# One decoder layer on one core: prompt keys of two heads in one 128-column product, the sixth latent block in two column halves, the first cached page on a semaphore of its own

## The chip, the cores and the metric

One Trainium2 chip, one of its NeuronCores. The metric is the time of one execution of the program on the device, in microseconds (us). Three runs of the kernel before were taken; their median is the number to compare with.

## The reference, cut to what matters

One decoder layer for 256 prompt positions and 8 single-token samples that share all weights. The part around the change is the latent attention:

```python
h = rmsnorm(x, lw['g_norm_mix']) * (1.0 + scale_m) + shift_m
p = jnp.einsum('ntd,de->nte', h, lw['w_in'])
q = mla_queries(p[..., OFF_Q:OFF_KV], pos, lw['g_q_lat'], lw['w_uq'], lw['g_qk_q'])
c_kv = rmsnorm(p[..., OFF_KV:OFF_KR], lw['g_kv_lat'])
k_rope = apply_rope(p[..., OFF_KR:OFF_CB], cos, sin)
...
def mla_keys(c_kv, k_rope, w_uk, g_qk_k):
    k_nope = jnp.einsum('...tc,chd->...thd', c_kv, w_uk)
    k_rot = jnp.broadcast_to(k_rope[..., None, :], k_nope.shape[:-1] + (QK_ROPE,))
    return rmsnorm(jnp.concatenate([k_nope, k_rot], axis=-1), g_qk_k)
```

With D_MODEL 1024, a query latent of 384, a key and value latent of 256, 8 heads, 64 unrotated and 32 rotated components per head. Each sample also attends to 8 cached pages of 128 latent rows. The layer ends with 64 routed experts of 3 MB each (float32), all of which are streamed from device memory.

## The kernel before, in words

All activations lie with features on the partitions and the 264 tokens (256 + 8) along the free axis. Everything is float32; each product in the program is recorded as two weight loads and two matmuls. Five engines run five programs that are written by hand and meet at semaphores. `STAGES` (L59) lists all products in the order in which TensorE makes them; each takes the next of four PSUM banks, and its number n gives the bank (n % 4) and how often it has been used. TensorE's `enter(n)` (L678) waits until the bank's last contents have been read, `full[n % 4]` tells the reader that it is filled, and `free[n % 4]` that it is read.

The order around the change is:

- **Early pages** (L416, L731, L1366, L1728). While the first weights load, the keys' squared lengths of 16 cached pages are made: SyncE issues the page loads in groups (`EGROUP`, L50), each group with one semaphore; TensorE waits for a group at its first page, and multiplies each page (2 products of 512 columns, 4 matmuls on record) by `wuk`; ScalarE squares, VectorE sums per head. Group 0 is pages 0 and 1 with `wuk`; group 1 is pages 2 and 3; group 2 is pages 4 and 5. Between them TensorE makes chunks of the conditioning (`ada_item`, L704, four column groups of 32 at once).
- **Latent blocks** (L763 to L778, stage `in0`). Six blocks of the combined projection, each 8 products of 264 columns over the 8 feature tiles of `hT`: three of queries, two of keys and values, and the sixth, the 32 rotated key components and their swapped copy, 64 output columns that are written to partitions 64 to 127. ScalarE copies each bank out (L1402, L1405) and squares the first five (L1411). Later VectorE rotates the sixth (`krT`, L1791 to L1793), after the variance of the query latent (L1786) and before the scaling of the query latent (L1797), which TensorE waits for ahead of stage `q`.
- **Prompt keys** (L824 to L831, stage `k`). For each of 8 heads 2 products of 64 output columns into a bank of its own; ScalarE copies each (L1449), and when all are there squares all heads in one instruction (L1455). TensorE goes on with four transposes (`ada_fold(6)`, L722), the sums of the squared queries (`qsum`), the values (`v`), and then the sums of the squared keys (`ksum`, L842), which wait for L1455.
- **After that** come the rest of the projection, attention with the cached pages, the branches, and the experts in pairs. SyncE's queue holds all large loads in program order, each behind a wait for TensorE to be done with the ring slot or chunk that it overwrites (L403, L408, L447, L548).

In the experts' `up` (L1236) two experts share one bank, each with 64 output columns, one on partitions 0 to 63 and one on 64 to 127, and the program goes from one to the other at each product.

Of the kernel before, what the change touches and what calls it, by code (L numbers as in the profile page):

```python
# [6 lines left out]
ALU = mybir.AluOpType  # L7
ACT = mybir.ActivationFunctionType
# [6 lines left out]
P = 128  # L15
D = 1024
DT = D // P
NP_ = 256
NS = 8
NT = NP_ + NS  # L20
NC = 1 + NS
H = 8
NOPE, ROPE = 64, 32
QK = NOPE + ROPE
QL, KL = 384, 256
QT, KT_ = QL // P, KL // P
# [18 lines left out]
T_Q, T_KV, T_CB, T_CC, T_CH, T_U, T_V = 0, 3, 5, 9, 13, 17, 21  # L45
# [1 line left out]

NPK = 6
EARLY = NS * (NPG - NPK)
EGROUP = (0, 2, 4, 6, 8, 10, 12, 16)  # L50

KNOW = []
for _q in range(NS):
# [2 lines left out]
BRANCH = []  # L56
for _m in range(DT):
    BRANCH += ([(f"bg{_m + 2}", 3)] if 0 < _m < DT - 2 else []) + [(f"bo{_m}", 3)]
STAGES = [("ek0", 2), ("ek2", 2), ("ada0", 1), ("ek4", 2), ("ek6", 2), ("norm1", 1), ("ada1", 1), ("ek8", 2), ("ada2", 1),  # L59
# [3 lines left out]
          ("ada10", 1), ("in_v2", 1), ("in_v3", 1), ("ada11", 1), ("know0", NPK // 2), ("self", 1), ("qlat", 1),  # L63
          ("know0b", 2), ("qlatT", 1), ("know0c", 1),
# [4 lines left out]
BASE = {}  # L69
# [110 lines left out]
def build(nc, A, O):  # L180

    with ExitStack() as ctx:
# [9 lines left out]
        hT = sb("hT", [P, DT, NT])  # L192
        xs = sb("xs", [P, 2, D + E])
        sq = xs[:].rearrange("p a c -> p (a c)")[:, 0:DT * NT].rearrange("p (k t) -> p k t", k=DT)
        pT = sb("pT", [P, NTILE, NT])
# [11 lines left out]
        krT = sb("krT", [P, 2, NT])  # L207
# [6 lines left out]
        kT = sb("kT", [P, H, NT])  # L214
# [12 lines left out]
        wuk = sb("wuk", [P, KT_, H * NOPE])[:]  # L227
# [118 lines left out]
        free = [sem(f"bank_free{i}") for i in range(4)]  # L346
# [330 lines left out]
        def _(pe):  # L677
# [14 lines left out]
            def mm(out, lhsT, rhs, start, stop):  # L692
                return nc.tensor.matmul(out, lhsT, rhs, start=start, stop=stop)  # L693
# [72 lines left out]
            w = part(0, 0, DT, 704)  # L766
            for m in range(6):
                n = BASE["in0"] + m
                t = enter(n)
                for k in range(DT):  # L770
                    if m == 0:
                        pe.wait_ge(s["h1"], k + 1)
                    if m < 5:
                        last = mm(t[:, 0:NT], w[:, k, m * P:(m + 1) * P], hT[:, k, :], k == 0, k == DT - 1)
                    else:
                        last = mm(t[NOPE:P, 0:NT], w[:, k, 640:704], hT[:, k, :], k == 0, k == DT - 1)
                last.then_inc(full[n % 4], 1)
            through(n, 0)  # L778

# [32 lines left out]
            for h in range(H):  # L812
                n = BASE["q"] + h
                t = enter(n)
                for k in range(QT):
                    last = mm(t[:, 0:NT], wuq[:, k, h * P:(h + 1) * P], pT[:, T_Q + k, :], k == 0, k == QT - 1)
# [5 lines left out]

            ada_item(6)
            pe.wait_ge(s["ckv"], 1)  # L824
            for h in range(H):
                n = BASE["k"] + h
                t = enter(n)
                for k in range(KT_):
                    last = mm(t[0:NOPE, 0:NT], wuk[:, k, h * NOPE:(h + 1) * NOPE], pT[:, T_KV + k, :],
                              k == 0, k == KT_ - 1)  # L830
                last.then_inc(full[n % 4], 1)  # L831
            ada_fold(6)
            pe.wait_ge(s["sqh"], 1)
# [1 line left out]
            for b in range(2):  # L835
                n = BASE["v"] + b
                t = enter(n)
                for k in range(KT_):
                    last = mm(t[:], pT[:, T_KV + k, b * P:(b + 1) * P], wuv[:, k, :], k == 0, k == KT_ - 1)
# [45 lines left out]
            n = BASE["self"]  # L885
            t = enter(n)
# [4 lines left out]
            n = BASE["qlat"]  # L891
            t = enter(n)
            for hf in range(2):
                for j in range(4):
                    h = 4 * hf + j
                    last = mm(t[32 * j:32 * j + NS, hf * KL:(hf + 1) * KL], qsg[0:NOPE, h, :], wukT[:, h, :], True, True)
# [3 lines left out]
            t = enter(m)  # L900
            pe.wait_ge(free[n % 4], n // 4 + 1)
            for k in range(KT_):
                for hf in range(2):
                    last = nc.tensor.transpose(t[:, (2 * k + hf) * P:(2 * k + hf + 1) * P],
                                               scr[:, (2 * hf + k) * P:(2 * hf + k + 1) * P], ident[:])
# [152 lines left out]
            for c in range(CT):  # L1058
                n = BASE["uvs"] + c
                t = enter(n)  # L1060
                for o in range(2):
                    h = 2 * c + o
                    for k in range(KT_):
                        last = mm(t[o * 64:(o + 1) * 64, 0:NS], wuv[:, k, h * NOPE:(h + 1) * NOPE], olat[:, k, h, :],
                                  k == 0, k == KT_ - 1)
# [8 lines left out]
            for m in range(DT):  # L1074
# [8 lines left out]
                for b in range(3):  # L1083
                    n = BASE[f"bo{m}"] + b
                    t = enter(n)
                    for k in range(CT):
                        last = mm(t[:, 0:NT], part(2 + hf, b * CT * 512, CT, 512)[:, k, (m % 4) * P:(m % 4 + 1) * P],
                                  src[b][:, k, :], k == 0, k == CT - 1)
# [4 lines left out]
            for m in range(DT):  # L1093
# [3 lines left out]
                n = BASE["out"] + m  # L1097
                t = enter(n)
                for k in range(DT):
                    if m == 0:  # L1100
                        pe.wait_ge(s["merged"], k + 1)
                    last = mm(t[:, 0:NT], part(b, 0, DT, 512)[:, k, (m % 4) * P:(m % 4 + 1) * P], mg[:, k, :],
                              k == 0, k == DT - 1)
# [21 lines left out]
            n = BASE["routT"]  # L1125
            t = enter(n)
            pe.wait_ge(s["lsig"], 1)
            for j, m in enumerate((P, P, NS)):
                last = nc.tensor.transpose(t[0:m, j * E:(j + 1) * E], lgT[:, j * P:j * P + m], ident[0:E, 0:E])
# [4 lines left out]
            for j, m in enumerate((P, P, NS)):  # L1134
                for hf in range(2):
                    x = 2 * j + hf
                    t = (pC, pD, pA)[x % 3]
# [3 lines left out]
                    for k in range(4):  # L1141
                        last = nc.tensor.transpose(t[0:m, k * P:(k + 1) * P], hT[:, 4 * hf + k, j * P:j * P + m], ident[:])
# [39 lines left out]
            for j, m in enumerate((P, P, NS)):  # L1182
                for i in range(j + 1):
                    kk = (P, P, NS)[i]
                    last = mm(pB[0:m, j * E:(j + 1) * E], (ones if i < j else tri)[0:kk, 0:m], ch[0:kk, i, :],
                              i == 0, i == j)
# [4 lines left out]
            n = BASE["posT"]  # L1191
            t = enter(n)
            for j, m in enumerate((P, P, NS)):
                last = nc.tensor.transpose(t[0:E, j * P:j * P + m], posm[0:m, j, :], ident[0:m, 0:m])
# [128 lines left out]
            with pe.If(over >= 1):  # L1323
                pe.wait_ge(s["fgates"], 1)
                n = BASE["fgates"]
                t = enter(n)
                for j, m in enumerate((P, P, NS)):
                    last = nc.tensor.transpose(t[0:E, j * P:j * P + m], ch[0:m, j, :], ident[0:m, 0:m])
# [19 lines left out]
        def _(act):  # L1348
# [8 lines left out]
            def fulls(n):  # L1357
                b, k = bank(n)
                act.wait_ge(full[b], k + 1)
                return bk[b]  # L1360
# [38 lines left out]
            for m in range(5):  # L1399
                n = BASE["in0"] + m  # L1400
                t = fulls(n)
                nc.scalar.activation(pT[:, m, :], t[:, 0:NT], ACT.Copy).then_inc(free[n % 4], 1)  # L1402
            n = BASE["in0"] + 5
            t = fulls(n)
            nc.scalar.activation(krT[NOPE:P, 0, :], t[NOPE:P, 0:NT], ACT.Copy).then_inc(free[n % 4], 1)  # L1405
            for b in range(4):
                act.wait_ge(free[b], (BASE["in0"] + 5 - b) // 4 + 1)
            act.sem_inc(s["krin"], 1)

            act.wait_ge(s["var1"], 1)  # L1410
            nc.scalar.activation(sq[:, 0:QT + KT_, :], pT[:, T_Q:T_Q + QT + KT_, :], ACT.Square).then_inc(s["sqq"], 1)  # L1411
# [22 lines left out]
            for h in range(H):  # L1434
                n = BASE["q"] + h
                t = fulls(n)
# [7 lines left out]
            mixed_rows("ch", (2, 3))  # L1444
            ada_rows((6,))
            for h in range(H):
                n = BASE["k"] + h
                t = fulls(n)
                nc.scalar.activation(kT[0:NOPE, h, :], t[0:NOPE, 0:NT], ACT.Copy).then_inc(free[n % 4], 1)  # L1449
            for n in range(BASE["k"] + 4, BASE["k"] + H):  # L1450
                act.wait_ge(free[n % 4], n // 4 + 1)
            act.wait_ge(s["kfull"], 1)
            act.wait_ge(s["ckv"], 1)
            act.wait_ge(s["z"], 1)
# [1 line left out]
            for b in range(2):  # L1456
                n = BASE["v"] + b
                t = fulls(n)
# [30 lines left out]
            n = BASE["qlat"]  # L1489
            t = fulls(n)  # L1490
# [52 lines left out]
            for q in range(NS):  # L1543
# [18 lines left out]
                o = 64 * (q % 2)  # L1562
# [14 lines left out]
                if q == 2:  # L1577
                    for b in range(2):
                        n = BASE["vtr"] + b
                        t = fulls(n)  # L1580
# [7 lines left out]
            for c in range(CT):  # L1588
                n = BASE["uvs"] + c
                t = fulls(n)  # L1590
# [22 lines left out]
            for j, m in enumerate((P, P, NS)):  # L1613
                for hf in range(2):
                    x = 2 * j + hf
# [21 lines left out]
            n = BASE["shgu1"]  # L1637
            t = fulls(n)
# [38 lines left out]
            with act.If(over >= 1):  # L1677
                n = BASE["fgates"]
                t = fulls(n)
# [12 lines left out]
        def _(dve):  # L1692
            chain = [0, c_dve]

            def link(ins):

                chain[0] += 1
                ins.then_inc(chain[1], 1)
                dve.wait_ge(chain[1], chain[0])

            def fulls(n):
                b, k = bank(n)
                dve.wait_ge(full[b], k + 1)
                return bk[b]

            V = nc.vector
# [79 lines left out]
            inv_var("cqn", QL, rstd[:])  # L1786
            dve.sem_inc(s["varlat"], 1)
            dve.wait_ge(d_late, 16 * 7)
            dve.wait_ge(s["krin"], 1)
            R, W = slice(NOPE, QK), slice(QK, P)  # L1790
            link(V.tensor_tensor(krT[R, 1, :], krT[W, 0, :], sinT[W, :], ALU.mult))  # L1791
            link(V.tensor_tensor(krT[R, 0, :], krT[R, 0, :], cosT[R, :], ALU.mult))
            link(V.tensor_tensor(krT[R, 1, :], krT[R, 0, :], krT[R, 1, :], ALU.add))  # L1793
# [2 lines left out]
            for k in range(QT):  # L1796
                last = V.scalar_tensor_tensor(out=pT[:, T_Q + k, :], in0=pT[:, T_Q + k, :],  # L1797
                                              scalar=vec[:, V_GQ + k:V_GQ + k + 1], in1=rstd[:],
                                              op0=ALU.mult, op1=ALU.mult)
# [70 lines left out]
            n = BASE["self"]  # L1870
            t = fulls(n)
# [5 lines left out]
            n = BASE["qlatT"]  # L1877
            t = fulls(n)
# [117 lines left out]
            for q in range(NS):  # L1996
# [30 lines left out]
                if q == 0:  # L2027

                    n = BASE["vmean"]
                    t = fulls(n)  # L2030
# [454 lines left out]
```

## Time and profile before

| | |
|---|---|
| median of 3 runs | 1022.16 us (1021.47 to 1022.84) |
| the profiled execution's own time | 1022.12 us |
| its span in the trace | 1020.4 us |
| TensorE (PE) busy | 978.8 us, 96% |
| VectorE (DVE) / ScalarE (ACT) busy | 610.4 us, 60% / 187.5 us, 18% |
| mean granted TensorE clock | 0.999 |
| moved by the DMA engines | 310.66 MB |

The span is the time between the first and the last instruction of the trace; 1.7 us of the execution lie outside of it. A busy matmul record includes its pipeline tail, so successive records overlap, and the distance between the starts is what a matmul costs. The profile's own lines are quoted in the section of rows.

### The profile page before, as it was taken

How to read it: one execution, taken by the hardware profiler on the slowest of the kernel's cores; microseconds unless marked ns; L12 is line 12 of the kernel's file. 1: busy time of each engine (PE TensorE's matmuls, PEld its weight loads, DVE VectorE, ACT ScalarE, POOL GpSimd, SP SyncE). 2: the span in 40 equal slices, each digit the busy share in tenths (PEclk: the TensorE clock that was granted, in tenths of full speed). 3: DMA queues.
4: the chain of work that ended last, by engine and by line, in shares of the span. 5: the costliest groups of instructions: out<-in, count | busy, mean ns of one | idle time of the engine just before them, and what ended most of it. 6: DMA issues, size and time to landing. Idle time of an engine off the chain costs nothing.

```text
span 1020.4 us, 14130 instructions
## 1 busy us (share of the span) xinstructions
PE 978.8 (96%) x4558; PEld 551.9 (54%) x4558; DVE 610.4 (60%) x1562; ACT 187.5 (18%) x384; POOL 56.7 (6%) x81
## 2 busy tenths in 40 slices
PE   6999999999999999999999999999999999999997
PEld 2477756544446788888744344444444344344443
DVE  3503322368764010123749889888888888888875
ACT  3311231345435100002510010000000010010000
POOL 0100001000000000000210000000000000000000
PEclk9999999999999999999999999999999999999999
DMA  8995459655536383544468999999999999999992
GB/s 314 419 368 206 173 172 327 207 154 175 169 104 258 127 358 135 206 145 185 169 227 336 417 427 423 426 425 422 425 426 423 424 426 423 425 421 425 423 393 73
DMA packets 53906, 310.66 MB, mean 304 GB/s; under 512 B 8810, under 2 KB 28298, under 8 KB 31842
## 3 DMA queue, kind: packets, MB, share of 16 engines
q1 hardware_dynamic: 47538, 296.13, 73.3%
q0 software_dynamic: 6320, 13.93, 3.9%
q8 instruction: 25, 0.41, 0.2%
q14 instruction: 23, 0.19, 0.1%
HBM read 315.80 MB, written 2.87 MB: 312 GB/s over the span
## 4 chain that ended last, share of the span: by engine, by line
PE 66%; DMA 26%; DVE 3%; issue 2%; SPq 1%; ACT 0%; DVEq 0%; PEldq 0%
PE bank L693 46%; DMA ring<-in_w_e_gu 25%; PE pA L693 15%; PE pB L693 2%; PE pC L693 2%; DMA pT<-in_poolT 1%; PE pD L693 1%; SPq L551 1%; PE pA L728 1%; DMA ring<-in_w_br 0%; PE pA L937 0%; DVE xT L2249 0%; PE pC L946 0%; DVE xT L2325 0%; SPq L414 0%
## 5 line engine op out<-in xcount | busy, mean ns | idle before, releaser
L693 PE MATMUL pA<-ring,qT 128*64 128x512 f32 x1008 | 226.8, 595 | 15.5 <-DMA ring<-in_w_e_gu 15.5
L2237 DVE STREAM_TRANSPOSE qT<-xs 32x256 f32<-32x256 f32 x480 | 209.2, 436 | 7.7
L693 PE MATMUL bank<-hT,ring 128*128 128x264 f32 (+1 forms) x832 | 191.1, 388 | 0.9 <-PE bank L693 0.9
L693 PEld LDWEIGHTS bank<-hT,ring 128*128 128x128 f32 (+1 forms) x832 | 155.4, 189 | 35.1 <-issue 8.7
L693 PEld LDWEIGHTS pA<-ring,qT 128*64 128x64 f32 x1008 | 76.2, 137 | 140.5 <-issue 131.6
L693 PE MATMUL bank<-pT,vtok 128*128 128x264 f32 x512 | 127.9, 393 | 0.3 <-DVE pT L2329 0.3
L693 PEld LDWEIGHTS bank<-pT,vtok 128*128 128x128 f32 x512 | 92.0, 190 | 39.3 <-issue 26.7
L2246 DVE TENSOR_TENSOR pT<-pT,bank 128x264 f32<-128x264 f32 x248 | 100.0, 427 | 8.8 <-PE bank L693 7.3
L693 PE MATMUL bank<-wuk,ring 128*128 128x512 f32 x192 | 86.3, 597 | 0.0
L693 PE MATMUL pB<-ring,oaT 128*64 128x512 f32 x252 | 62.0, 605 | 0.0
L693 PE MATMUL pC<-ring,oaT 128*64 128x512 f32 x252 | 60.4, 592 | 0.0
L693 PEld LDWEIGHTS bank<-wuk,ring 128*128 128x128 f32 x192 | 35.0, 190 | 41.6 <-issue 41.0
L660 POOL DMA_INDIRECT xs<-h_rows,idx x32 | 31.9, 998 | 429.2 <-DVE sinT L2226 418.3
L1659 ACT ACTIVATE oaT<-pA 128x256 f32<-128x256 f32 x32 | 12.3, 384 | 229.4 <-PE pA L693 229.4
L693 PE MATMUL bank<-pT,ring 128*128 128x264 f32 (+1 forms) x208 | 48.6, 388 | 0.0
L1665 ACT ACTIVATE vtok<-pC 128x512 f32<-128x512 f32 x32 | 19.1, 598 | 158.5 <-PE pC L693 158.5
L1832 DVE TENSOR_REDUCE xs<-ksq 128x8 f32<-128x512 f32 x48 | 32.3, 685 | 23.7 <-ACT ksq L1483 21.9
L2074 DVE TENSOR_TENSOR pT<-bank,pT 128x264 f32<-128x264 f32 x18 | 7.8, 433 | 61.9 <-PE bank L693 61.9
L693 PEld LDWEIGHTS bank<-pT,ring 128*128 128x128 f32 x208 | 39.3, 190 | 7.3 <-issue 0.4
L693 PE MATMUL bank<-wuk,pT 128*128 128x512 f32 x64 | 31.0, 635 | 9.0 <-DMA pT<-in_poolT 7.8
L693 PE MATMUL bank<-qT,ring 128*128 128x264 f32 x160 | 36.6, 388 | 1.2 <-PE bank L693 0.6
L693 PEld LDWEIGHTS pC<-ring,oaT 128*64 128x64 f32 x252 | 18.4, 137 | 35.4 <-issue 35.4
(323 smaller groups left out, 779.8 us busy)
## 6 DMA issues: line engine op xcount, KB each, us to landing
ring<-in_w_e_gu SPq DMA_DIRECT2D x63, 2048.0 KB, 23.0
ring<-in_w_e_dn SPq DMA_DIRECT2D x63, 1024.0 KB, 18.5
ring<-in_poolT SPq DMA_DIRECT2D x64, 208.0 KB, 2.7
ring<-in_w_ada SPq DMA_DIRECT2D x12, 1024.0 KB, 9.9
ring<-in_w_bg SPq DMA_DIRECT2D x4, 3072.0 KB, 11.8
ring<-in_w_mix SPq DMA_DIRECT2D x5, 2048.0 KB, 14.7
ring<-in_w_ada SPq DMA_DIRECT2D x4, 2048.0 KB, 13.0
ring<-in_poolR SPq DMA_DIRECT2D x56, 128.0 KB, 2.1
```

The lines of the kernel that those rows point to most:

```text
L551: sp.dma_start(part(place(e)[0], 0, DT, 2 * FE), one("w_e_gu", e if i is None else i * 4 + e)).then_inc(wgt[place(e)[0]], 16)
L660: nc.gpsimd.indirect_dma_start(out=xs[:, q % 2, :], out_offset=None, in_=h2rows, in_offset=bass.IndirectOffsetOnAxis(ap=idx[:, q % 2:q % 2 ...
L693: return nc.tensor.matmul(out, lhsT, rhs, start=start, stop=stop)
L728: last = nc.tensor.transpose(pA[:, m * P:(m + 1) * P], adb[:, x % 2, m * P:(m + 1) * P], ident[:])
L1659: nc.scalar.activation(silu_s, pA[:, 0:FE], ACT.Silu).then_inc(s["silu_s"], 1)
L1665: nc.scalar.activation(yrow[:, 512:], pC[:], ACT.Copy).then_inc(s["y1"], 1)
L1832: V.tensor_reduce(out=kss[:, q, j, :], in_=ksq[:, j % 2, :].rearrange("p (h d) -> p h d", h=H), op=ALU.add, axis=AX.X).then_inc(s["ksq_use ...
L2074: link(V.tensor_tensor(g[:, b, :], t[:, 0:NT], g[:, b, :], ALU.mult))
L2237: last = V.transpose(xTs[32 * j:32 * j + 32, q % 2, :, 32 * a:32 * a + 32], src[32 * a:32 * a + 32, j])
L2246: V.tensor_tensor(yacc[:, m, :], yacc[:, m, :], bk[n % 4][:, 0:NT], ALU.add).then_inc(free[n % 4], 1)
```

## The change

The semaphore of early group 0 now covers page 0 and `wuk`; group 1 is pages 1, 2 and 3. The order of the loads stays. The sixth latent block alternates between two column halves: feature tiles of even number go to partitions 64 to 127, those of odd number to 0 to 63. ScalarE copies both halves to partitions 64 to 127 of the two planes of `krT`, and a new VectorE addition joins them ahead of the rotation. Stage `k` makes four products of 128 columns, two heads each; ScalarE still makes eight copies of 64 partitions, of which every second reads partitions 64 to 127 and writes 0 to 63, and frees a bank after its second copy has ended.

```diff
-EGROUP = (0, 2, 4, 6, 8, 10, 12, 16)
+EGROUP = (0, 1, 4, 6, 8, 10, 12, 16)
...
-STAGES = [("ek0", 2), ("ek2", 2), ...
+STAGES = [("ek0", 1), ("ek1", 3), ...
-          ... ("k", 8), ("qsum", 1), ("v", 2), ("ksum", 1), ...
+          ... ("k", 4), ("qsum", 1), ("v", 2), ("ksum", 1), ...
@@ tensor, sixth latent block @@
-                        last = mm(t[NOPE:P, 0:NT], w[:, k, 640:704], hT[:, k, :], k == 0, k == DT - 1)
+                        o = NOPE * (1 - k % 2)
+                        last = mm(t[o:o + NOPE, 0:NT], w[:, k, 640:704], hT[:, k, :], k < 2, k >= DT - 2)
@@ tensor, prompt keys @@
-            for h in range(H):
-                n = BASE["k"] + h
+            for h2 in range(H // 2):
+                n = BASE["k"] + h2
                 t = enter(n)
                 for k in range(KT_):
-                    last = mm(t[0:NOPE, 0:NT], wuk[:, k, h * NOPE:(h + 1) * NOPE], pT[:, T_KV + k, :],
-                              k == 0, k == KT_ - 1)
+                    last = mm(t[:, 0:NT], wuk[:, k, h2 * P:(h2 + 1) * P], pT[:, T_KV + k, :], k == 0, k == KT_ - 1)
                 last.then_inc(full[n % 4], 1)
@@ scalar, sixth latent block @@
-            nc.scalar.activation(krT[NOPE:P, 0, :], t[NOPE:P, 0:NT], ACT.Copy).then_inc(free[n % 4], 1)
+            for x in range(2):
+                nc.scalar.activation(krT[NOPE:P, x, :], t[NOPE * (1 - x):NOPE * (1 - x) + NOPE, 0:NT], ACT.Copy
+                                     ).then_inc(s["krin"], 1)
+            act.wait_ge(s["krin"], 2)
+            act.sem_inc(free[n % 4], 1)
             for b in range(4):
                 act.wait_ge(free[b], (BASE["in0"] + 5 - b) // 4 + 1)
-            act.sem_inc(s["krin"], 1)
@@ scalar, prompt keys @@
-                n = BASE["k"] + h
-                t = fulls(n)
-                nc.scalar.activation(kT[0:NOPE, h, :], t[0:NOPE, 0:NT], ACT.Copy).then_inc(free[n % 4], 1)
-            for n in range(BASE["k"] + 4, BASE["k"] + H):
-                act.wait_ge(free[n % 4], n // 4 + 1)
+                n = BASE["k"] + h // 2
+                if h % 2 == 0:
+                    t = fulls(n)
+                o = NOPE * (h % 2)
+                nc.scalar.activation(kT[0:NOPE, h, :], t[o:o + NOPE, 0:NT], ACT.Copy).then_inc(s["qcopy"], 1)
+                if h % 2:
+                    act.wait_ge(s["qcopy"], H + h + 1)
+                    act.sem_inc(free[n % 4], 1)
@@ vector, ahead of the rotation @@
-            dve.wait_ge(s["krin"], 1)
+            dve.wait_ge(s["krin"], 2)
             R, W = slice(NOPE, QK), slice(QK, P)
+            link(V.tensor_tensor(krT[NOPE:P, 0, :], krT[NOPE:P, 0, :], krT[NOPE:P, 1, :], ALU.add))
             link(V.tensor_tensor(krT[R, 1, :], krT[W, 0, :], sinT[W, :], ALU.mult))
```

## Rows read from the trace of the kernel before

**Rows 1.** Chain that ended last, in order: start us, us, what (xcount).

```profile
10.38 8.50 DMA pT<-in_poolT
19.02 7.12 PE bank L693 x16
...
44.89 26.67 PE bank L693 x108
71.85 14.49 PE bank L693 x64
...
132.70 9.19 PE bank L693 x48
...
639.15 7.04 PE pA L693 x32
646.89 22.08 DMA ring<-in_w_e_gu
```

**Rows 2.** Windows A:B: length, PE, PEld, DVE, ACT, POOL busy (instructions), clock, DMA share, GB/s.

```profile
510.00:520.00 10.00, 9.45 (x42) 7.25 (x41) 7.23 (x26) 0.00 (x0) 2.21 (x3) 1.00 0.12 31
...
560.00:580.00 20.00, 20.00 (x93) 8.57 (x93) 17.29 (x43) 1.58 (x5) 0.99 (x1) 1.00 1.00 414
```

**Rows 3.** Timeline, first pages: start us, us, instruction, idle before it.

```profile
3.47 3.63 SPq L419 DMA_DIRECT2D pT<-in_poolT  x4
...
6.80 9.31 PE L693 MATMUL bank<-wuk,pT 128*128 128x512 f32 x16 [6.80 <-DMA pT<-in_poolT]
```

**Rows 4.** Line L419: landing of the page issued at 3.5, then of that at 6.8.

```profile
DMA to landing us min/median/max: 2.8/2.8/2.8
...
DMA to landing us min/median/max: 2.1/2.1/2.1
```

**Rows 5.** ScalarE's timeline: copies of the fifth and the sixth latent block.

```profile
67.88 0.39 ACT L1402 ACTIVATE pT<-bank 128x264 f32<-128x264 f32 x1 [3.17 <-PE bank L693]
71.58 0.39 ACT L1405 ACTIVATE krT<-bank 64x264 f32<-64x264 f32 x1 [3.31 <-PE bank L693]
```

**Rows 6.** VectorE's timeline: rotation of the key part, scaling of the query latent.

```profile
89.96 0.43 DVE L1791 TENSOR_TENSOR krT<-krT,sinT 32x264 f32<-32x264 f32 x1 [0.22 <-DVE rstd L1714]
90.42 0.42 DVE L1792 TENSOR_TENSOR krT<-krT,cosT 32x264 f32<-32x264 f32 x1
...
91.47 1.30 DVE L1797 SCALAR_TENSOR_TENSOR pT<-pT,vec,rstd 128x264 f32<-128x264 f32 x3 [0.16 <-DVE krT L1793]
```

**Rows 7.** TensorE's timeline: queries, prompt keys, transposes, sums of squared keys.

```profile
104.82 10.85 PE L693 MATMUL bank<-pT,ring 128*128 128x264 f32 x48
...
134.56 7.33 PE L693 MATMUL bank<-pT,wuk 128*64 128x264 f32 x32
141.82 0.66 PE L728 MATMUL pA<-ident,ksq 128*128 128x128 f32 x4
...
147.07 1.10 PE L693 MATMUL bank<-pT,onecol 96*32 96x264 f32 x16
```

**Rows 8.** ScalarE's timeline: copies of the first, second and last head, the squares.

```profile
135.70 0.38 ACT L1449 ACTIVATE kT<-bank 64x264 f32<-64x264 f32 x1 [0.42 <-PE bank L693]
136.59 0.39 ACT L1449 ACTIVATE kT<-bank 64x264 f32<-64x264 f32 x1 [0.51 <-PE bank L693]
...
141.93 0.38 ACT L1449 ACTIVATE kT<-bank 64x264 f32<-64x264 f32 x1 [0.51 <-PE bank L693]
142.55 1.97 ACT L1455 ACTIVATE pT<-kT 96x2112 f32<-96x2112 f32 x1 [0.24 <-ACT kT L1449]
```

**Rows 9.** Line L406, chunk 8's loads: ns min/median/max, first and last start, landing.

```profile
L406 SPq DMA_DIRECT2D ring<-in_w_ada x2: 433/1059/1685, 141.2 to 143.0; - x2
...
DMA to landing us min/median/max: 6.3/6.7/7.1
```

**Rows 10.** TensorE's timeline: conditioning chunk 8.

```profile
157.57 1.92 PE L693 MATMUL bank<-ring,csig 128*32 128x512 f32 x16
```

**Rows 11.** TensorE's timeline: spatial products, 64 columns, two in a row on one half.

```profile
266.48 1.99 PE L693 MATMUL bank<-ring,pT 128*64 128x128 f32 x32 [0.26 <-issue]
```

More of the change, by code:

```diff
@@ L58 @@
     BRANCH += ([(f"bg{_m + 2}", 3)] if 0 < _m < DT - 2 else []) + [(f"bo{_m}", 3)]
-STAGES = [("ek0", 2), ("ek2", 2), ("ada0", 1), ("ek4", 2), ("ek6", 2), ("norm1", 1), ("ada1", 1), ("ek8", 2), ("ada2", 1),
+STAGES = [("ek0", 1), ("ek1", 3), ("ada0", 1), ("ek4", 2), ("ek6", 2), ("norm1", 1), ("ada1", 1), ("ek8", 2), ("ada2", 1),
           ("ek10", 2), ("ada3", 1), ("ek12", 4), ("in0", 6), ("in_cb", 4), ("cqn", 1), ("kvn", 1), ("ada4", 1),
[1 row of a table removed]
[1 row of a table added]
           ("ada8", 1), ("in_u2", 1), ("in_u3", 1), ("ada9", 1), ("in_v", 2),
```

2 rows, old and new, of the table STAGES are left out of this document.

## The prediction, made before the changed kernel had run

> **What bounds the kernel now.** I read the chain of work that ended last first, because TensorE is busy for 96% of the span and a busy share does not say what a microsecond saved on it is worth. The reader is to see two regimes. From 44.89 us on the chain is TensorE almost without a break: the block that holds the sixth latent block (44.89 to 71.56), the next piece from 71.85, the piece with the prompt keys from 132.70 [rows 1]. From 646.89 on the chain is the experts' weights, 22 to 24 us of transfer for each 7 us of TensorE [rows 1]. So the second question is whether a microsecond saved in the first regime reaches the end of the second. The windows answer it: between 510 and 520 us the DMA engines are busy 0.12 of the time, between 560 and 580 fully, at 414 GB/s [rows 2]. The stream has no backlog at 510; it is started and refilled by SyncE behind waits for TensorE (L535, L549). If TensorE gets there earlier, the stream starts and ends earlier by as much. Savings ahead of 510 us therefore count in full, unless something between is tied to a time that TensorE does not set.
>
> **First page on its own semaphore.** TensorE starts at 6.80, when page 1 lands; the four first pages are issued from 3.47 in 3.63 us, so about 1.1 us apart, the last at 6.77 [rows 3]. Page 0 lands 2.8 us after its issue, at 6.3 [rows 4]; that is the new start, 0.5 us earlier. Page 1 now waits for pages 1 to 3, and page 3 lands at 6.77 + 2.1 = 8.9 [rows 4]. Page 0's four matmuls run at the lower clock: the first 16 take 9.31 us [rows 3] against 7.12 for 16 later ones [rows 1], 2.2 us more, which is five at twice 0.43 us. So page 0 keeps TensorE until 6.3 + 4 x 0.86 = 9.7, and the new wait costs nothing. But the 0.5 us goes nowhere: the chain shows that pages 4 and 5 land at 10.38 + 8.50 = 18.88, and TensorE resumes at 19.02 [rows 1]. SyncE issues those pages without waiting for TensorE. I take 0; bounds 0 and -0.5 us. What hides it is that landing; what grows is the idle time ahead of 19.02, from 1.05 to 1.55 us.
>
> **Sixth latent block.** ScalarE's copies follow TensorE: the fifth block's begins at 67.88, the sixth's at 71.58 [rows 5], 3.70 us for 16 matmuls of 264 columns, of which about 0.14 us is the change to 64 columns (below). A matmul is thus 3.56 / 16 = 0.223 us. Whether two column halves run side by side can be read from the experts, where the same order is used: 32 matmuls of 64 by 512 columns in 7.04 us, 0.22 each, where 16 full-width ones take 7.12 us, 0.445 each [rows 1]. Two run in the time of one. So 16 matmuls become 8 steps: 8 x 0.223 = 1.78 us saved, on the chain. The bounds are 0 (no overlap) and 1.78 (no two halves can do more); I take 1.78, as the experts' row is the same pattern on the same engine.
>
> By the Trainium skill (TensorE: Matmul & The Clock Gate, Measured speedup vs the span model) three column tiles gave 2.38 times the speed, 79% of the ideal. By that two would give 1.59, the block would save 1.3 us, and the sum below would be 0.5 us smaller; the experts' row, 7.12 against 7.04 us for twice the matmuls, disagrees.
>
> What it adds: a second ScalarE copy (0.39 us) and a wait for both before the bank is freed. Behind them in ScalarE's queue is the squaring and then the next copy, and ScalarE sits idle for over 3 us ahead of each copy here [rows 5]; the variance that needs the squares is made only behind the next 64 matmuls. VectorE gets one more addition in its chain. Its neighbours of this size take 0.42 to 0.43 us [rows 6], so 0.46 with the link; behind it waits the scaling of the query latent, done at 92.8, which TensorE wants at 104.82 [rows 6, 7]: 12 us of cover. The stored rotated key on GpSimd's queue comes 0.5 us later beside that, and nobody on the chain waits for it. All 0.
>
> **Prompt keys.** 32 matmuls from 134.56; the copies of two heads are 0.89 us apart [rows 7, 8], that is four matmuls at 0.223. Eight heads are 7.12 us, and the next work would stand at 141.68; it stands at 141.82 [rows 7], the 0.14 us being the change from 64 columns to 128. After the change there are 16 matmuls, 3.56 us, and keys and transposes have the same width. Saved: 3.56 + 0.14 = 3.70 us; bounds 3.56 and 3.70.
>
> Does ScalarE keep up? Product j is full at 135.70 + 0.89 j, so the last at 138.37. Two copies are 0.38 each; with a semaphore round trip of about 0.2 (ScalarE's step from the last copy to the squares is 0.24, [rows 8]) a product costs ScalarE about 0.9 us, just TensorE's pace. Its last copy ends near 139.3, the squares run from 139.5 to 141.5 instead of 142.55 to 144.5. TensorE asks for them ahead of the sums at 147.07 - 3.70 = 143.4 [rows 7]. 1.9 us of cover remains; late next would be exactly this wait. Banks: the queries' sums and the values reuse the banks of products 0 to 2, which are free 1 us and more before.
>
> The Trainium skill speaks against this (TensorEngine Tiling (Array Packing), PSUM Bottleneck): a faster TensorE leaves the emptying of PSUM as it was, so the copies may become the bound. Here the rows say that they come level with TensorE, not behind; the case in which they fall behind is a rival below.
>
> **What does not move with TensorE.** SyncE issues the cached pages and behind them conditioning chunk 8; these follow the `ch` weights, so they move by 1.78 only, while their user moves by 5.48. The last load of chunk 8 starts at 143.0 and lands 7.1 us later, at 150.1 [rows 9], after the change 148.3. TensorE wants the chunk at 157.57 - 5.48 = 152.1 [rows 10]. 3.8 us of cover. The later chunks are issued behind a wait for TensorE and move with it.
>
> **Sum.** 0 - 1.78 - 3.70 = -5.48 us. The profiled execution took 1022.12 us (span 1020.4 and 1.7 around it), which is the median, 1022.16, within 0.04. So 1022.16 - 5.48 = 1016.7 us. Its own range is 1015.9 to 1017.5: 0.5 us of the page and the runs' scatter of 0.7 on either side.
>
> **Rivals.**
> *The halves do not overlap* (the block doesn't do what it says): -3.70 only, 1018.5 us. For it: the spatial products, also 64 columns wide, take 1.99 us for 32 of 128 columns [rows 11], 0.06 each, which is 128 columns at full clock with nothing side by side. Against it: there two products of one half follow each other, here the halves alternate, as in `up`. 5%.
> *The copies stay the pace*: if ScalarE still needs 0.89 us per head, the squares end at 144.5, TensorE asks at 143.4 and loses about 1.3 us with the handing over: 1018.0 us. For it: each pair now ends in a round trip. Against: 0.38 us a copy. 8%.
> *The longer idle ahead of page 4 drops the clock*: five matmuls more at the lower level, 2.2 us as at the start: 1018.9 us. Against: before, 1.05 us of idle left it up. 4%.
> *Slower*: four key copies now read partitions 64 to 127 and write 0 to 63. No ScalarE row shows this. A VectorE operation that moves by 32 partitions costs 0.43 us against 0.42 for one that doesn't [rows 6], so I expect nothing. But if a crossing copy took 3.4 us rather than 0.38, four would add 12 us, the cover takes 1.9, and 10.2 - 5.5 = +4.7 gives 1026.9 us. It decides from (1.9 + 5.5) / 4 = 1.85 us extra a copy. 3%.
> *No change*: the time saved is waited out between 150 and 510 us, at a load that I take to follow TensorE but that doesn't: 1022.2 us. Against: the chain shows transfers there only at the branch weights, and SyncE issues them behind TensorE. 4%.
>
> **Numbers.** The forecast holds 76%. The measurement can tell about 0.2%, 2 us, from no change; all cases but the last two are faster by more. The range 1015.7 to 1018.7 leaves out the last two, half of the clock's case and the tail of the first.
>
> **What would show it.** Key matmuls x16 in about 3.8 us with 128*128 in the record; the sixth block's copy 1.9 us, not 3.7, behind the fifth's; no wait of TensorE ahead of the sums of squared keys; TensorE still resuming at 19.0 with page 4; every mark after the keys, the start of the expert stream included, 5.5 us earlier. A sixth block of 3.6 us, a TensorE wait for L1455, or matmuls of page 4 at 0.86 us would make me wrong, and so would marks 5.5 us early at 500 us with an unmoved end.

## The result and the profile after

The changed kernel takes 1016.05 us (median of 4, 1015.97 to 1016.44) against 1022.04 us for the kernel before (median of 4, 1021.47 to 1022.84): 5.99 us less, a ratio of 0.9942 with a 95% interval of 0.9926 to 0.9958. Run again beside nine runs of the kernel before it took 1016.13 us against 1021.87. The forecast was 1016.7 us, 5.48 us less.

The profiled execution of the changed kernel took 1016.44 us with a span of 1014.7 us. Its chain of work that ended last (start us, us, what):

```profile
10.55 7.82 DMA pT<-in_poolT
18.50 7.12 PE bank L693 x16
...
44.37 24.91 PE bank L693 x108
69.57 14.49 PE bank L693 x64
...
130.45 5.68 PE bank L693 x32
136.57 11.16 PE bank L693 x72
...
450.83 14.49 PE bank L693 x64
...
633.25 7.04 PE pA L693 x32
640.99 21.88 DMA ring<-in_w_e_gu
```

Set beside [rows 1], the marks move in three steps. Page 4 starts at 18.50 instead of 19.02: 0.52 us. The piece behind the latent blocks starts at 69.57 instead of 71.85: 2.28 us, 1.76 more. From there the piece with chunk 6 and the keys moves with them (130.45 against 132.70). The keys are the third step, told below: at the sums of their squares, 141.16 against 147.07 [rows 7], the difference is 5.91 us. At the first experts in the transfer-bound stretch, 633.25 against 639.15, it is 5.90 us. Both kernels then need 381.3 us, give or take 0.1, to the end of the span (1020.4 - 639.15 = 381.25; 1014.7 - 633.25 = 381.45). Nothing is given back by the stream of weights.

Between the keys and the stream the difference is not constant. It is 5.66 us at 450.83, where the chain of the kernel before has

```profile
456.49 14.49 PE bank L693 x64
```

and it is back at 5.90 from 506.63 on (512.53 before), mainly since the chain before has 0.43 us of issue at 510.96 where the changed kernel's has 0.08 at 505.30. So the 5.90 of two single traces is good to about 0.25 us.

The windows before and in the stream, the same stretches as in [rows 2] moved by 6 us, agree with the reason that was forecast: the DMA engines are as idle ahead of it (0.11) and as full in it (1.00).

```profile
504.00:514.00 10.00, 9.69 (x43) 7.56 (x43) 7.48 (x26) 0.00 (x0) 2.14 (x2) 1.00 0.11 30
554.00:574.00 20.00, 20.00 (x92) 8.57 (x90) 17.29 (x43) 1.58 (x5) 0.99 (x1) 1.00 1.00 413
```

TensorE's timeline of the changed kernel, the latent blocks and the keys to the sums of the squared keys:

```profile
49.36 19.89 PE L693 MATMUL bank<-hT,ring 128*128 128x264 f32 x96
69.57 14.48 PE L693 MATMUL bank<-hT,ring 128*128 128x264 f32 x64 [0.31 <-PE bank L693]
...
132.30 3.83 PE L693 MATMUL bank<-pT,wuk 128*128 128x264 f32 x16
135.97 0.60 PE L728 MATMUL pA<-ident,ksq 128*128 128x128 f32 x4
136.50 1.10 PE L693 MATMUL bank<-xs,onecol 96*32 96x264 f32 x16
137.53 3.70 PE L693 MATMUL bank<-ring,pT 128*128 128x512 f32 x8
141.16 1.10 PE L693 MATMUL bank<-pT,onecol 96*32 96x264 f32 x16
```

From the first key to the sums of squared keys it is 8.86 us; before it was 147.07 - 134.56 = 12.51 [rows 7], so another 3.65 us are saved. No row between shows a wait. ScalarE beside it:

```profile
67.36 0.39 ACT L1402 ACTIVATE pT<-bank 128x264 f32<-128x264 f32 x1 [3.17 <-PE bank L693]
69.30 0.79 ACT L1406 ACTIVATE krT<-bank 64x264 f32<-64x264 f32 x2 [1.55 <-PE bank L693]
...
133.50 3.54 ACT L1454 ACTIVATE kT<-bank 64x264 f32<-64x264 f32 x8 [0.47 <-PE bank L693]
137.24 1.96 ACT L1461 ACTIVATE pT<-kT 96x2112 f32<-96x2112 f32 x1 [0.20 <-ACT kT L1454]
```

The sixth block's copy begins 1.94 us behind the fifth's, not 3.70 as in [rows 5]. The eight head copies take 3.54 us in all, 0.44 each, those that read partitions 64 to 127 and write 0 to 63 included (387 ns in the single records, 384 for the others), and the squares end at 139.2, 2.0 us before TensorE asks for them at 141.16.

### The profile page after: what moved, and what is told of

Read it like the earlier page. It is cut to its first block, busy times and chain, and to the rows that moved or that the text cites. A ratio compares the mean times of both kernels' runs of the same rounds, so it can differ in the third digit from the quotient of the medians.

```text
span 1014.7 us, 14103 instructions
## 1 busy us (share of the span) xinstructions
PE 973.0 (96%) x4542; PEld 549.4 (54%) x4542; DVE 610.8 (60%) x1563; ACT 188.0 (19%) x385; POOL 56.6 (6%) x81
## 3 DMA queue, kind: packets, MB, share of 16 engines
HBM read 315.80 MB, written 2.87 MB: 314 GB/s over the span
## 4 chain that ended last, share of the span: by engine, by line
PE 66%; DMA 27%; DVE 3%; issue 2%; SPq 1%; ACT 0%; DVEq 0%; PEldq 0%
PE bank L693 45%; DMA ring<-in_w_e_gu 25%; PE pA L693 15%; PE pB L693 2%; PE pC L693 2%; DMA pT<-in_poolT 1%; PE pD L693 1%; SPq L551 1%; PE pA L728 1%; DMA ring<-in_w_br 0%; PE pA L937 0%; DVE xT L2256 0%; PE pC L946 0%; DVE xT L2332 0%; SPq L414 0%
```

## The experiments

**Each part alone, and all without the page.** Three kernels made one part of the change, a fourth all but the semaphore groups.

```diff
 # page_only, on the kernel before
-EGROUP = (0, 2, 4, 6, 8, 10, 12, 16)
+EGROUP = (0, 1, 4, 6, 8, 10, 12, 16)
 # halves_only: the hunks of L776, L1405 and L1789 alone
 # keys_only: the hunks of L61, L825 and L1446 alone
 # all_but_page: halves_only and keys_only together
```

> Only the semaphore groups of the early pages are changed. Theory A (pages 4 and 5 set the time, TensorE resumes when they land whatever it did before): TensorE starts near 6.2 us instead of 6.8, the idle time ahead of page 4 grows by what is saved, the time stays at 1022.0 within 0.3. Theory B (part of the change's 6.0 us comes from here, since the landing of pages 4 and 5 was seen 0.5 us earlier in the changed kernel): 1021.5, with page 4 starting at 18.5 instead of 19.0.

> Only the sixth latent block in two column halves. Theory A (two halves side by side, 8 steps of 0.223 us saved, all of it on the chain): 1.76 us less, 1020.3; the two copies of the block begin 1.9 us behind the copy of the fifth. Theory B (halves don't overlap): 1022.0.

> Only the prompt keys as four products of 128 columns. Theory A (16 matmuls and one change of width saved): 3.65 us less, 1018.4, and no wait of TensorE ahead of the sums of the squared keys. Theory B (ScalarE's copies stay the pace, TensorE waits for the squares): about 2.4 us less, 1019.6.

> The whole change without the new semaphore groups of the early pages. Theory A: as the changed kernel, 1016.1 within 0.3, if the landing of pages 4 and 5 varies by itself. Theory B: 0.5 us more, 1016.6. If both parts add up with nothing lost, 1022.0 - 1.76 - 3.65 = 1016.6 as well, so the page-only run decides what the rest is.

Beside 21 runs of the kernel before (median 1022.09):

| kernel | us | less than before | ratio, 95% interval |
|---|---|---|---|
| page_only | 1021.86 | 0.23 | 0.9999 (0.9990 to 1.0008) |
| halves_only | 1019.93 | 2.16 | 0.9980 (0.9971 to 0.9989) |
| keys_only | 1018.47 | 3.62 | 0.9965 (0.9951 to 0.9978) |
| all_but_page | 1016.95 | 5.14 | 0.9948 (0.9934 to 0.9961) |

The keys are 3.62 us where 3.70 was forecast. The halves' median is 0.4 us more than their term, but their 11 runs reach from 1019.74 to 1020.76 us, and the profiled one, 1020.33, is 1.79 less than the profiled one before. Its trace shows the term itself: latent blocks from 49.78 to 69.99, 20.21 us, as in the changed kernel (49.36 to 69.57), against 21.97 before (TensorE's timeline and the chain). The page alone cannot be told from nothing.

What varies from one trace to the next is the start. TensorE's timeline in four of the traces, with the page's own semaphore in the changed kernel and in changed_again (the same kernel, below), without it in the last two (halves_only, all_but_page):

```profile
6.24 8.84 PE L693 MATMUL bank<-wuk,pT 128*128 128x512 f32 x16 [6.24 <-DMA pT<-in_poolT]
...
18.50 7.10 PE L693 MATMUL bank<-wuk,pT 128*128 128x512 f32 x16 [1.56 <-DMA pT<-in_poolT]
```

```profile
6.11 9.92 PE L693 MATMUL bank<-wuk,pT 128*128 128x512 f32 x16 [6.11 <-DMA pT<-in_poolT]
...
18.54 7.11 PE L693 MATMUL bank<-wuk,pT 128*128 128x512 f32 x16 [0.65 <-DMA pT<-in_poolT]
```

```profile
6.93 9.62 PE L693 MATMUL bank<-wuk,pT 128*128 128x512 f32 x16 [6.93 <-DMA pT<-in_poolT]
18.74 7.11 PE L693 MATMUL bank<-wuk,pT 128*128 128x512 f32 x16 [0.33 <-DMA pT<-in_poolT]
```

```profile
6.88 9.72 PE L693 MATMUL bank<-wuk,pT 128*128 128x512 f32 x16 [6.88 <-DMA pT<-in_poolT]
18.79 7.10 PE L693 MATMUL bank<-wuk,pT 128*128 128x512 f32 x16 [0.33 <-DMA pT<-in_poolT]
```

Three things are to be seen. The first is that the same kernel needs 8.84 us for its first 16 matmuls once and 9.92 another time. In the single records the starts of these matmuls lie 0.85 us apart or a little more up to the fifth in the one trace and up to the seventh in the other, and 0.43 us apart from soon after: the clock rises from its lower level to the higher after a different number of them.

The second is page 4's start. It lies between 18.5 and 18.9 with the new groups (18.50, 18.85, 18.63, 18.83, 18.79, 18.54 in six traces) and between 18.7 and 19.0 without them (19.02, 18.74, 18.92, 18.79 in four). The means are 18.69 and 18.87. Mostly the landing of pages 4 and 5 sets it, but not in halves_only and all_but_page: there the pages have landed by 18.51 and 18.56, and page 4 starts 0.23 us later, 0.33 us behind the conditioning chunk. The same gap stands behind the next chunk (ahead of 28.91 in halves_only), where no page is waited for. In these two traces TensorE is the later of the two.

The third is that page 4 is not the only way by which the start reaches the rest. The chain of halves_only does not pass through the landing of the pages:

```profile
6.93 11.52 PE bank L693 x32
...
18.96 1.96 ACT xs L1389
20.95 4.00 DVE rstd L1740
...
28.04 1.81 DVE rstd L1718
```

It goes from TensorE's start to the end of conditioning chunk 0, to ScalarE's copy of that chunk, to the squares of the activations behind it in ScalarE's queue, and to VectorE's sum and inverse of them, which the norm ahead of the latent blocks needs. The chains of all_but_page and copies_plus8 do the same. When TensorE starts earlier, this path ends earlier, and the landing of pages 4 and 5 hides nothing of it.

What both paths leave is read at the first latent matmul. It stands at 49.31 to 49.53 us in the six traces with the new groups (mean 49.44) and at 49.61 to 49.88 in the four without them (mean 49.78). The two sets do not overlap, and the difference is 0.34 us, with the landings' own scatter in it. So the page's semaphore is worth about 0.3 us in the traces, not 0. Its median alone, 0.23 us, cannot tell that from nothing, and theory A holds for page_only within what the runs can tell.

all_but_page, at 1016.95, came 0.35 us above what its theory B gave and 0.9 above the changed kernel, with intervals that overlap. In its trace the latent blocks start 0.47 us later than in the changed kernel's (49.83 against 49.36) and the span is 0.4 us longer; whether the rest of the 0.9 is more than scatter stays open.

**The same halves, one after the other.**

```diff
-                        o = NOPE * (1 - k % 2)
-                        last = mm(t[o:o + NOPE, 0:NT], ..., k < 2, k >= DT - 2)
+                        o = NOPE * (1 - k // 4)
+                        last = mm(t[o:o + NOPE, 0:NT], ..., k % 4 == 0, k % 4 == 3)
```

> The changed kernel, but the sixth block's feature tiles 0 to 3 go to the upper half one after another and then 4 to 7 to the lower, so that the same two halves are used without alternating. Theory A (two halves run side by side only where matmuls for both are near each other in the queue): the block takes 3.5 us again, the sixth copy begins about 3.5 us behind the fifth's and the time is 1.5 to 1.8 us above the changed kernel's, 1017.7. Theory B (the engine looks far enough ahead that the order doesn't matter): 1016.1, the copy 1.9 us behind.

1017.47 us (ratio to before 0.9956, 0.9941 to 0.9971), 1.42 above the changed kernel by the medians; the profiled execution took 1017.04 us. ScalarE's timeline of that kernel:

```profile
67.31 0.39 ACT L1402 ACTIVATE pT<-bank 128x264 f32<-128x264 f32 x1 [3.17 <-PE bank L693]
70.18 0.79 ACT L1406 ACTIVATE krT<-bank 64x264 f32<-64x264 f32 x2 [2.48 <-PE bank L693]
```

The copy begins 2.87 us behind the fifth's: between the 1.94 us of the alternating order and the 3.70 of one half. Neither theory is right. At 0.223 us a step, 2.87 - 1.94 is 4 steps above the 8 of the alternating order, so 12 steps for 16 matmuls: the second half's first four ran beside the first half's last four. The single records agree: the starts come one by one up to 67.93 us and in twos from 68.15, where the fifth of the first half is due. Alternating is worth 0.9 us of the part's 1.76; the rest comes in this order too.

**How much cover ScalarE has.** Extra copies, each with a wait behind it, ahead of heads 0 and 2 (copies_plus2), or of all eight (copies_plus8):

```diff
+                if h in (0, 2):
+                    link(nc.scalar.activation(kT[0:NOPE, h, :], t[o:o + NOPE, 0:NT], ACT.Copy))
                 nc.scalar.activation(kT[0:NOPE, h, :], t[o:o + NOPE, 0:NT], ACT.Copy).then_inc(s["qcopy"], 1)
```

> The changed kernel with two more copies in ScalarE's queue (heads 0 and 2 are copied twice, with a wait between, about 0.6 us each). Theory A (1.9 us of cover ahead of the sums of the squared keys): the squares end 1.2 us later, TensorE does not wait, 1016.1. Theory B (ScalarE is the pace already): 1.2 us more, 1017.3.

> The changed kernel with every one of the eight head copies made twice. Theory A: ScalarE needs about 8 x 1.05 = 8.4 us for them, the squares end near 144.1 in the changed kernel's trace, TensorE asks at 141.2 and waits 3 us: 1019.1. If the cover were larger than thought (or the squares not what is waited for), less: 1016.1 to 1018.

1016.14 us (ratio 0.9940, 0.9925 to 0.9955) and 1017.81 us (0.9958, 0.9943 to 0.9973): nothing, and 1.76 us more than the changed kernel. In copies_plus2 the squares begin at 138.19, 0.95 us later than in the changed kernel, and TensorE does not wait. The rows of copies_plus8, ScalarE's squares and TensorE's next step:

```profile
140.66 1.96 ACT L1463 ACTIVATE pT<-kT 96x2112 f32<-96x2112 f32 x1 [0.20 <-ACT kT L1456]
```

```profile
142.68 1.10 PE L693 MATMUL bank<-pT,onecol 96*32 96x264 f32 x16 [1.37 <-ACT pT L1463]
```

Theory A's mechanism holds: the wait is at L842, on the squares. Its size was too large because an extra copy costs about 0.42 us in the timeline (starts at 133.58, 134.00, 134.40), not 1.05 - 0.45 = 0.6. The squares moved by 140.66 - 137.24 = 3.42 us, less 0.08 us for the later start of the keys, and of that 2.0 us was cover and 1.37 became a wait. So the cover is 2.0 us, measured by using it up. The other 0.4 us between the medians is not accounted for by this wait.

**Two tries at the start.** The first loads pages 4 and 5 and the activations ahead of conditioning chunk 0 and multiplies those pages ahead of it; the second puts pages 4 to 7 and the column sum of the norm ahead of the chunk.

```diff
 # start_reordered, SyncE (TensorE, ScalarE and STAGES to match)
             early_pages(1)
-            ada_item(0)
+            early_pages(2)
             ... xT, vec
-            early_pages(2)
+            ada_item(0)
 # start_pages_then_chunk, SyncE (the others to match)
             early_pages(1)
-            ada_item(0)
             ... xT, vec
             early_pages(2)
             early_pages(3)
+            ada_item(0)
```

> The changed kernel with pages 4 and 5 loaded right behind pages 0 to 3 and multiplied ahead of the first conditioning chunk, and the activations loaded and squared ahead of that chunk. Theory A (what binds the start is the landing of pages 4 and 5 behind 3 MB of other loads, with nothing close behind it): the first 24 matmuls run without a break, the norm's column sum comes 1.5 us earlier and the time falls to 1014.5. Theory B (something is just behind: the first chunk's weights, which now land later, or VectorE's sum of squares): 1015.5 to 1016.5.

> The changed kernel with the activations loaded behind pages 0 to 3, then pages 4 to 7, and only then the first conditioning chunk; TensorE multiplies all eight pages and the norm's column sum and then the chunk. The first reordering ended in a wait for the chunk's weights (landed at 19.6). Theory A (loads are what spaces the start, and TensorE has work enough to cover them in this order): eight pages without a break from 6.3 to 22.7, the second chunk at 25.6 instead of 26.4, one wait of 0.35 us for VectorE less: 0.8 to 1.2 us less than the changed kernel, 1015.0. Theory B (another thing is just as late, VectorE's sum of squares or a later load): 1016.0.

> The changed kernel once more, word for word, beside the reordered one and more runs of the kernel before. Theory A: 1016.05 within 0.3, and page 4 starts between 18.4 and 18.9 us, since nothing else is between. If the first look was a lucky one, 1016.6.

1016.33 us, 1015.93 us and 1016.13 us, ratios 0.9942, 0.9943 and 0.9943, each within 0.0015 either way: none differs from the changed kernel by more than the scatter of the runs. TensorE's timeline of start_reordered:

```profile
6.36 13.09 PE L693 MATMUL bank<-wuk,pT 128*128 128x512 f32 x24 [6.36 <-DMA pT<-in_poolT]
19.73 1.92 PE L693 MATMUL bank<-ring,csig 128*32 128x512 f32 x16 [0.28 <-DMA ring<-in_w_ada]
21.98 3.67 PE L693 MATMUL bank<-wuk,pT 128*128 128x512 f32 x8 [0.32 <-PE bank L693]
25.49 0.61 PE L693 MATMUL bank<-rstd,ones 128*128 128x264 f32 x2
```

and of start_pages_then_chunk:

```profile
6.83 16.10 PE L693 MATMUL bank<-wuk,pT 128*128 128x512 f32 x32 [6.83 <-DMA pT<-in_poolT]
23.00 0.68 PE L693 MATMUL bank<-rstd,ones 128*128 128x264 f32 x2
23.61 1.92 PE L693 MATMUL bank<-ring,csig 128*32 128x512 f32 x16
26.25 0.66 PE L728 MATMUL pA<-ident,ksq 128*128 128x128 f32 x4 [0.72 <-ACT ksq L1383]
```

In the first the wait for pages became a wait for the chunk's weights, and the column sum stands at 25.49 where changed_again has 25.48. In the second TensorE runs through to 25.5, and the next gap is a wait of 0.72 us for ScalarE to copy the chunk out, work that other work used to cover. The latent blocks start at 49.06 us there, against 49.36 and 49.43: 0.3 us, where 0.8 to 1.2 was expected. But this trace began late: its page 0 landed at 6.79, later than in any other trace here (6.07 to 6.47), and its chain is TensorE almost alone from there to the latent blocks. With page 0 at 6.2 it would have stood some 0.6 us better (an estimate), so the trace does not refute theory A; the median of five runs, 1015.93, shows no such gain either.

## Why the prediction was right, point by point

- **What bounds the kernel.** Right. The marks move by 5.90 us at the start of the transfer-bound stretch, give or take the 0.25 that is lost and found again on the way, and the rest takes as long as before. The DMA engines' idle stretch ahead of the stream was the row that carried this.
- **Sixth block, 1.78 us.** Measured 1.76 in the traces (21.97 to 20.21), 2.16 by the medians of halves_only. The experts' row was the right precedent. The Trainium skill's figure for three column tiles (TensorE: Matmul & The Clock Gate, Measured speedup vs the span model), carried over to two, would have given an estimated 1.3 us; these traces disagree, as two halves ran at twice the rate of one. The rival in which the halves don't overlap fell, and the row that spoke for it, [rows 11], had been misread. The prediction took 0.06 us a matmul for the full-width rate of 128 columns. But four transposes of 128 columns at full width take 0.44 us in the chain before, 0.11 each:

```profile
44.45 0.44 PE pA L728 x4
```

So the spatial products, two of one half and then two of the other (four matmuls on record each), already ran two at a time, and the row was evidence for the block. halves_in_turn, in which four matmuls of one half ran beside four of the other, agrees.
- **Prompt keys, 3.70 us.** Measured 3.65 in the traces, 3.62 by the medians, within the bounds of 3.56 and 3.70.
- **ScalarE's cover of 1.9 us.** Measured 2.0, by the rows and by the extra copies. The rivals of copies that stay the pace and of slow crossing copies fell: a crossing copy takes as long as a straight one. The Trainium skill's remark that tiling does not speed up the emptying of PSUM (TensorEngine Tiling (Array Packing), PSUM Bottleneck) agrees with these traces as a margin, not as a bound: 0.44 us of ScalarE a head against 0.445 of TensorE.
- **First page, 0.** This is the term that was mis-sized: about 0.3 us, by the first latent matmul in ten traces. "The 0.5 us goes nowhere" is true of one path, page 4, and only where the pages land later than TensorE comes back. The step left out a second path, from the end of conditioning chunk 0 through ScalarE's squares to the norm, which moves with TensorE's start. The two traces compared here differ by 0.52 us at page 4, which with 1.76 and 3.65 makes the 5.9 of the marks; most of that 0.52 is luck, since pages 4 and 5 landed at 18.36 in the one and at 18.88 in the other, and in the other traces anywhere between. Of the 0.5 us by which the forecast fell short, 0.3 is thus this term, and the rest is within the scatter of the runs. The idle time grew from 1.05 to 1.56 us as forecast, and page 4 then ran at the higher clock: 7.12 us for 16 matmuls, as before, so the clock's rival fell.
- **What does not move with TensorE.** Right in that conditioning chunk 8 started at 151.66 without a wait, but its sizes were off on the safe side: its last load landed at 146.6 (issued at 139.62), 3.5 us earlier than before and not 1.78, so the cover was 5.1 us and not 3.8. And the step named only this transfer, where there was a nearer one, told below.

## What to carry to other kernels

Before crediting a saving ahead of a transfer-bound phase, look for a stretch between in which the DMA engines are nearly idle. Here there was one, and the saving passed through whole. In this kernel, matmuls of 64 output columns took half the time when they went to the two column halves in turn, with 128, 264 and 512 moving columns; where two products share the moving operand, one product of 128 columns makes both in the time of one, as the keys show. What a faster producer does to its reader is read as a margin: the time from the reader's end to the next engine's request, here 2.0 us, which took in two more copies and not eight. And before a saving is written off as hidden by one wait, follow the other engines' work that starts behind the same instruction.

## What the runs showed that was not expected

**A transfer that lost its cover.** VectorE's normalisation of the queries waits for the heads' norms to come back from memory. Its row in the changed kernel, and what follows:

```profile
164.58 2.41 DVE L1853 SCALAR_TENSOR_TENSOR qT<-qT,gqp,xs 96x2112 f32<-96x2112 f32 x1 [6.46 <-DMA xs<-head_norms]
167.03 0.23 DVE L1861 COPY xs<-kss_e 128x128 f32<-128x128 f32 x1
167.88 0.31 DVE L1758 TENSOR_REDUCE ada<-pA 128x36 f32<-128x144 f32 x1 [0.62 <-PE pA L728]
169.72 2.42 DVE L1853 SCALAR_TENSOR_TENSOR kT<-kT,vec,pT 96x2112 f32<-96x2112 f32 x1 [1.54 <-DMA pT<-head_norms]
```

Before, it stood here:

```profile
164.95 2.42 DVE L1846 SCALAR_TENSOR_TENSOR qT<-qT,gqp,xs 96x2112 f32<-96x2112 f32 x1 [0.91 <-DMA xs<-head_norms]
```

All around it moved by 5.9 us, this row by 0.4. The wait is 7.96 us in changed_again, 7.60 in all_but_page and 7.18 in keys_only, but 0.53 in halves_only and 0.45 in page_only. That looks as if the keys made it, yet copies_plus8 has the keys as well and waits only 1.25 us. What separates the traces is the order of two transfers: GpSimd's load of the norms (L622), which waits for four small stores to land, and SyncE's next conditioning loads (L406), which wait for TensorE. In GpSimd's and SyncE's timelines they begin, before, in the changed kernel and in copies_plus8, at:

```profile
158.38 0.53 POOL L622 DMA_DIRECT2D xs<-head_norms  x1 [3.21 <-DMA head_norms<-abuf]
159.56 0.81 SPq L406 DMA_DIRECT2D ring<-in_w_ada  x2
```

```profile
153.65 0.82 SPq L406 DMA_DIRECT2D ring<-in_w_ada  x2
153.89 0.53 POOL L622 DMA_DIRECT2D xs<-head_norms  x1 [4.65 <-DMA head_norms<-abuf]
```

```profile
154.01 0.53 POOL L622 DMA_DIRECT2D xs<-head_norms  x1 [3.23 <-DMA head_norms<-abuf]
155.16 0.81 SPq L406 DMA_DIRECT2D ring<-in_w_ada  x2
```

In four traces (before, page_only, halves_only, copies_plus8) the load of the norms is issued 1.1 to 1.2 us ahead of the conditioning loads, and it lands 6.1 to 6.9 us after its issue. In the other eight it is issued between 0.02 us ahead of them and 0.7 behind, and it lands 10.7 to 13.3 us after its issue. The order changed because the conditioning loads move with TensorE by the whole 5.9 us and the load of the norms by 4.5 only: the last of its four stores took 6.9 us to land in the changed kernel where it had taken 5.4. Why that store takes longer is not shown, and no run changed the order of the two transfers alone.

It costs nothing yet, since TensorE needs these results more than ten microseconds later. But where 0.62 us of idle time is left here ahead of the next fold (L1758), changed_again has none: its fold starts behind the normalisation, at 168.84.

**The order of halves matters only in part**, as shown by halves_in_turn: 12 steps, not 16, when eight matmuls for one half precede eight for the other. The spatial products, four and four, lose nothing once they run: 32 of them in 1.99 us [rows 11].
